# Rows of x turned by a diagonal of their norms inside the projections, and half of the output weight split before attention

## What is computed

```python
hn   = rms_norm(x, attn_norm_gain)          # x * rsqrt(mean(x*x)) * gain, per token
proj = hn @ w_in                            # 1024 x 3072: q, k, v (4 heads) and c, u, b of the conv
q, k = partial_rotary(rms_norm(q)), partial_rotary(rms_norm(k))
attn = diff_attention(q, k, v)              # two softmax maps per head, p0 - lam * p1, then norm
conv = rms_norm(b * causal_conv3(c * u), conv_out_gain)
x    = x + concat(attn, conv) @ w_out       # 1024 x 1024
x    = x + hier_moe(rms_norm(x, ffn_norm_gain))   # 32 experts, two per token
```

## Time and profile before

| | us |
|---|---|
| median of 3 runs | 1182.52 (1179.73 to 1183.26) |
| profiled execution, its own time | 1183.22 |
| profiled execution, span of the core | 1181.4 |
| PE busy | 1106.2 (94% of the span) |
| DVE busy | 841.2 (71%) |
| ACT busy | 657.1 (56%) |
| POOL busy | 354.9 (30%) |
| TensorE clock granted, mean of the span | 0.978 of full |

### The profile page before, as it was taken

The page is one execution under the profiler, slowest core; times in us unless marked ns, Lnnn a source line. Parts: engine busy times, 40 slices in busy tenths (PEclk is TensorE's granted clock), DMA queues, the critical chain, the costliest instruction groups (busy, mean ns, idle before and its releaser), DMA issues.

```text
span 1181.4 us, 15242 instructions
## 1 busy us (share of the span) xinstructions
PE 1106.2 (94%) x5629; PEld 867.1 (73%) x5629; DVE 841.2 (71%) x1110; ACT 657.1 (56%) x901; POOL 354.9 (30%) x431
## 2 busy tenths in 40 slices
PE   4999999999879999989789999999999999999995
PEld 3998989889658877767657777777777777766663
DVE  6644354343587776766669899889889889888894
ACT  5412121111366555443348778778877877777773
POOL 2432333233311111112104433344344344222220
PEclk9999999999899999999789999999999999999998
DMA  8012030300510222322789999999999999999972
GB/s 243 17 47 61 19 90 1 89 19 18 195 6 19 89 90 90 126 90 98 268 302 355 380 369 373 380 373 366 382 375 369 377 354 356 372 365 360 368 309 44
DMA packets 76506, 254.16 MB, mean 215 GB/s; under 512 B 17808, under 2 KB 42384, under 8 KB 51856
## 3 DMA queue, kind: packets, MB, share of 16 engines
q1 hardware_dynamic: 69264, 236.37, 54.0%
q0 software_dynamic: 7168, 16.79, 6.0%
HBM read 240.55 MB, written 20.97 MB: 221 GB/s over the span
## 4 chain that ended last, share of the span: by engine, by line
PE 43%; DMA 7%; DVE 3%; ACT 1%; issue 1%; POOL 0%; POOLq 0%; SPq 0%; ACTq 0%; DVEq 0%
PE banks L2070 9%; PE banks L2072 9%; PE banks L2071 9%; PE banks L2089 4%; PE banks L2091 4%; PE banks L2087 4%; DMA raw<-in_w_up 3%; DMA raw<-in_w_gate 3%; PE banks L2046 2%; DVE wlo L1991 1%; PE banks L2055 1%; DMA rows<-xn_rows,table_i 1%; ACT whi L1940 1%; DMA xn_rows<-hn 0%; PE banks L1611 0%
## 5 line engine op out<-in xcount | busy, mean ns | idle before, releaser
L1991 DVE TENSOR_TENSOR wlo<-raw,whi 128x2048 fp32r<-128x2048 f32 x190 | 428.0, 2287 | 52.2 <-ACT whi L1940 52.0
L1940 ACT CAST whi<-raw 128x2048 fp32r<-128x2048 f32 x188 | 354.0, 1910 | 39.0 <-DMA raw<-in_w_gate 23.5
L2070 PE MATMUL banks<-whi,rT_hi 128*96 128x512 f32 x512 | 206.9, 404 | 7.1 <-DVE wlo L1991 6.1
L1922 POOL DMA_INDIRECT out<-y_sb,table_i x32 | 150.5, 4702 | 198.1 <-ACT y_sb L1958 192.9
L2072 PE MATMUL banks<-whi,rT_lo 128*96 128x512 f32 x512 | 203.0, 396 | 0.0
L2071 PE MATMUL banks<-wlo,rT_hi 128*96 128x512 f32 x512 | 201.8, 394 | 0.0
L2070 PEld LDWEIGHTS banks<-whi,rT_hi 128*96 128x96 f32 x512 | 83.1, 162 | 43.2 <-DVE wlo L1991 7.2
L2072 PEld LDWEIGHTS banks<-whi,rT_lo 128*96 128x96 f32 x512 | 82.9, 162 | 36.4
L1913 POOL DMA_INDIRECT rows<-xn_rows,table_i x30 | 52.4, 1745 | 188.7 <-PE banks L2046 181.1
L2071 PEld LDWEIGHTS banks<-wlo,rT_hi 128*96 128x96 f32 x512 | 83.4, 163 | 31.4
L847 ACT ACTIVATE qk_sq<-banks 128x256 f32<-128x256 f32 x32 | 12.3, 385 | 150.0 <-PE banks L1469 150.0
(11 more groups left out here) (248 smaller groups left out, 2051.1 us busy)
## 6 DMA issues: line engine op xcount, KB each, us to landing
raw<-in_w_gate SPq DMA_DIRECT2D x64, 1024.0 KB, 22.1
raw<-in_w_up SPq DMA_DIRECT2D x64, 1024.0 KB, 22.4
raw<-in_w_down SPq DMA_DIRECT2D x64, 1024.0 KB, 23.6
c_raw<-in_w_in SPq DMA_DIRECT2D x12, 512.0 KB, 3.8
q_raw<-in_w_in SPq DMA_DIRECT2D x12, 512.0 KB, 6.0
x_stage<-in_x SPq DMA_DIRECT2D x8, 512.0 KB, 7.7
wo_raw<-in_w_out SPq DMA_DIRECT2D x2, 2048.0 KB, 10.4
h_sb<-in_x SPq DMA_DIRECT2D x8, 512.0 KB, 4.6
```

The lines of the kernel that those rows point to most:

```text
L1922: pool.indirect_dma_start(out=s.out_rows, out_offset=bass.IndirectOffsetOnAxis(ap=s.table_i[:, e:e + 1], axis=0), in_=s.y_sb[e % 2][:], in ...
L1940: act.copy(s.w_hi[i % HI][:], s.raw[i % RING][:]).then_inc(s.hi_ready, 1)
L1991: dve.tensor_tensor(s.w_lo[i % RING][:], s.raw[i % RING][:], s.w_hi[i % HI][:].bitcast(F32), ALU.subtract).then_inc(s.lo_ready, 1)
L2070: pe.matmul(o, s.rT_hi[e % 2][:, c, :], hi[:, c4, :], start=(c == 0), stop=False)
```

## The change

It does five things.

- The tile of x is turned as it is: `turn_x` multiplies the raw tile, as weights, with a diagonal matrix of 1/rms (`diag_x`, made by POOL from the identity), eight plain float32 matmuls in place of eight transposes. DVE's `normalise` is gone. The gain moves into the weights: ACT rounds `gain * w` and DVE subtracts, one instruction for each of the eight row chunks (`gain1_c[:, c]` is a scale per partition), so `round_q` and `low_q` have eight pieces of 384 columns in place of four of 768, and `round_c` and `low_c` eight of 128 in place of one of 1024.
- Only tile 0 is turned ahead of the products. Projection 0 comes first, and the PE waits for its weights chunk by chunk. Tiles 1, 2, 3, 4 and 6 are turned within projections 0 to 4, tiles 5 and 7 within units 0 and 1. One pair of PSUM banks (4 and 5) serves all turns.
- `UNIT_AFTER`: units 0 and 1 stand after projections 3 and 4, units 18 to 22 after 24 to 28; only unit 23 is left behind projection 31, split around `turn_q(0)`.
- The conv half of `w_out` is loaded after unit 22 and its four chunks are split at projections 30 and 31 and just behind; `multiply_out(0, 0)` and `(0, 1)` move from slots 4 and 5 to slots 0 and 1. The attention half is split in slots 2 to 5, one chunk in a slot.
- POOL makes the first four `q_dup` ahead of the last square; `sum_conv` writes bank 1.

```diff
-UNIT_AFTER = (-1, 2, 5, 6, 7, 7, 9, 11, 13, 14, 15, 15, 17, 19, 21, 22, 23, 23, 25, 26, 28, 29, 31, 31)
+UNIT_AFTER = (3, 4, 5, 6, 7, 7, 9, 11, 13, 14, 15, 15, 17, 19, 21, 22, 23, 23, 24, 25, 26, 27, 28, 31)
+    def turned_in(p):
+        return {0: 1, 1: 2, 2: 3, 3: 4, 4: 6}.get(p)
+    def turned_in_unit(n):
+        return {0: 5, 1: 7}.get(n)
     def fill_at(g):
+        if g < 2:
+            return 0, g
         i, q = g // HEADS - 1, g % HEADS
-        return (i, q) if 0 <= i < NT else (None, None)
+        return (i, q) if 0 <= i < NT and (i > 0 or q >= 2) else (None, None)
     def chunks_at(g):
-        return [(4, 5), (6, 7), (0, 1), (2, 3)][g - 2] if 2 <= g < 6 else ()
+        return (g - 2,) if 2 <= g < 6 else ()
...
             def rstd_x(t):
...
-                pool.tensor_tensor(s.rstd_x[:, t:t + 1], s.ss_x[:, t:t + 1], s.neg_half[:, t:t + 1], ALU.pow).then_inc(x_rstd_ready, 1)
+                own.then(pool.tensor_tensor(s.rstd_x[:, t:t + 1], s.ss_x[:, t:t + 1], s.neg_half[:, t:t + 1], ALU.pow))
+                if t >= 2:
+                    pool.wait_ge(x_turned, t - 1)
+                pool.tensor_scalar(s.diag_x[t % 2][:], ident[:], s.rstd_x[:, t:t + 1], None, ALU.mult).then_inc(diag_ready, 1)
...
             def round_c(j):
...
-                act.copy(s.c_hi[j % 2][:], s.c_raw[j % 2][:]).then_inc(c_hi_ready, 1)
+                for c in range(KC):
+                    act.activation(s.c_hi[j % 2][:, c, :], s.c_raw[j % 2][:, c, :], ACT.Identity,
+                                   scale=s.gain1_c[:, c:c + 1]).then_inc(c_hi_ready, 1)
...
             def low_c(j):
-                dve.wait_ge(c_hi_ready, j + 1)
-                dve.tensor_tensor(s.c_lo[j % 2][:], s.c_raw[j % 2][:], s.c_hi[j % 2][:].bitcast(F32),
-                                  ALU.subtract).then_inc(c_lo_ready, 1)
+                dve.wait_ge(c_hi_ready, KC * (j + 1))
+                for c in range(KC):
+                    dve.scalar_tensor_tensor(s.c_lo[j % 2][:, c, :], s.c_raw[j % 2][:, c, :], s.gain1_c[:, c:c + 1],
+                                             s.c_hi[j % 2][:, c, :].bitcast(F32), ALU.mult, ALU.subtract).then_inc(c_lo_ready, 1)
...
             def turn_x(t):
                 a, _ = x_banks(t)
-                pe.wait_ge(xn_ready, t + 1)
-                if t >= 2:
-                    pe.wait_ge(xlo_ready, t - 1 if t < 5 else t)
+                pe.wait_ge(diag_ready, t + 1)
+                if t >= 1:
+                    pe.wait_ge(xlo_ready, t)
                 for c in range(KC):
-                    ins = pe.transpose(ps[:, a + c // 4, (c % 4) * P:(c % 4 + 1) * P], s.xn[t % 2][:, c * P:(c + 1) * P], ident[:])
+                    ins = pe.matmul(ps[:, a + c // 4, (c % 4) * P:(c % 4 + 1) * P], s.x_stage[t][:, c * P:(c + 1) * P], s.diag_x[t % 2][:],
+                                    start=True, stop=True)
...
             def project(p):
...
-                pe.wait_ge(q_lo_ready, PIECES * (h + 1))
                 for c in range(KC):
+                    if t == 0:
+                        pe.wait_ge(q_lo_ready, KC * h + c + 1)
+                    if c == (4 if p == 0 else 2) and turned_in(p) is not None:
+                        turn_x(turned_in(p))
...
             pe.wait_ge(consts, 3)
-            for t in range(4):
-                turn_x(t)
-            multiply_unit(0)
+            turn_x(0)
             for p in range(PROJ):
                 project(p)
-                if p < 4:
-                    turn_x(4 + p)
...
-            multiply_unit(UNITS - 2)
             turn_k(PROJ - 2)
+            multiply_unit(UNITS - 1, (0,))
             turn_q(0)
-            multiply_unit(UNITS - 1, (0,))
+            multiply_unit(UNITS - 1, (1,))
             turn_k(PROJ - 1)
+            turn_q(1)
             for g in range(SLOTS_2):
...
-                if g == 0:
-                    turn_q(1)
-                    multiply_unit(UNITS - 1, (1,))
```

More of the change, by code:

```diff
@@ L179, in layer_kernel @@
         x_stage = [at(f"x_stage{t}", 76 + 8 * (NT - 1 - t), [P, D]) for t in range(NT)]
-        xn = [at(f"xn{b}", 72 + 8 * b, [P, D]) for b in range(2)]
-        gain1 = at("gain1", 88, [P, D])
+        diag_x = [at(f"diag_x{b}", 72 + 8 * b, [P, P]) for b in range(2)]
+        gain1_c = at("gain1_c", 3.8125, [P, KC])
         squares = at("squares", 96, [P, D])
@@ L211, in layer_kernel @@
         ma_hi = [at(f"ma_hi{b}", 172 + 2 * b, [P, HEADS, P], F32R) for b in range(2)]
[L212 to L214 removed]
+        ma_lo = [at(f"ma_lo{b}", 180 + 2 * b, [P, HEADS, P], F32R) for b in range(2)]
+        mc_hi = at("mc_hi", 176, [P, CT, P], F32R)
+        mc_lo = at("mc_lo", 178, [P, CT, P], F32R)
         h_sb = [at(f"h_sb{b}", 184 + 4 * b, [P, D]) for b in range(2)]
@@ L362, in front @@
     taps_in = sem("taps_in")
-    x_in = [sem(f"x_in{n}") for n in range(5)]
+    x_in = [sem(f"x_in{n}") for n in range(NT)]
     qw_in = sem("qw_in")
@@ L467, in units_after @@
     def units_after(p):
-        return [n for n in range(1, UNITS) if UNIT_AFTER[n] == p]
+        return [n for n in range(UNITS) if UNIT_AFTER[n] == p]
     def split_after(n):
@@ L608, in _ @@
                 sp.dma_start(s.sub_gain[:], s.subln_gain.rearrange("a p -> p a")).then_inc(small_in, 16)
-                for t in range(4, NT):
+                load_x(2)
+                load_x(3)
+                load_c(0)
+                load_x(4)
+                load_c(1)
+                for t in range(5, NT):
                     load_x(t)
-                load_c(1)
                 for m in range(CT):
@@ L790, in _ @@
                     rstd_o(g - 2)
[L791 removed]
+                if 2 <= g and g + 2 < SLOTS_2:
                     double_q(g + 2)
@@ L832, in round_q @@
                     act.wait_ge(projected, NT * h)
-                for n in range(PIECES):
-                    act.copy(piece(s.q_hi, n), piece(s.q_raw, n).rearrange("p c j n -> p c (j n)")).then_inc(q_hi_ready, 1)
+                if h == 0:
+                    act.wait_ge(gain1_in, 16)
+                for c in range(KC):
+                    act.activation(s.q_hi[:, c, :], s.q_raw[:, c, :, :].rearrange("p j n -> p (j n)"), ACT.Identity,
+                                   scale=s.gain1_c[:, c:c + 1]).then_inc(q_hi_ready, 1)
             def round_c(j):
```

223 lines of the change are left out of this document (109 added, 114 removed).

## The result

The changed kernel takes **1190.74 us** (median of 5 runs, 1188.48 to 1192.74), the kernel before 1182.38 beside it on the same chip. The ratio is 1.0072, 95% interval 1.0049 to 1.0095: slower by 0.7%, 8.4 us between the medians. A second measurement of the same kernel gave 1.0070 (1.0045 to 1.0096). The profiled execution took 1190.74 with a span of 1189.0, that is 7.6 over the profiled span of before (1181.4).

The account below looks back on a forecast made before the run. The PE was taken to bound the projections, with room for gain in the head and at the start of attention. Terms summed to +2.5 on 1183.22: 1185.7 profiled, 1185.0 median, own range 1180 to 1189, wide range 1176 to 1192.

Parts of the forecast that it names:

- Start of the products: Head: the first product starts at 14.75 instead of 24.07 us, -9.3.
- Turns: Among the products: seven turns of sixteen records each instead of four turns of 0.79, +9.3.
- First projections: Projections 0 to 3: PE waits for diagonals and low parts behind ACT's pieces, +2.6 (bounds 1 and 5).
- Tile 7: Unit 1, behind projection 4: PE waits 3.5 for the diagonal, plus 1.2 for half a chance of slow clock, +4.7.
- Conv blocks: Five units wait for low parts of conv blocks made in eight pieces, +5.1 (bounds 0 and 8).
- The rival that they do not bite: The five conv waits and tile 7's are covered, so 9.8 goes: 1175.2; chance 0.22.
- Head weights: Heads 1 to 3: by chunks, the PE no longer waits for the last piece of low weights, -3.6.
- Start of attention: From projection 31's end to slot 6's turn: 50.8 without the moved unit becomes 43.5, less give-backs, -6.3 (bounds 2 and 11).
- they only shift: Experts from 600 us on: untouched by the change, their loads start where attention ends, so they only move in time.
- The rival of the clock: PE runs at 1.2 GHz behind waits in projections 0 to 3, tile 7, slots 1 to 5: +6, 1191; chance 0.20.

Follow-up runs that it names:

- silu_first: Changed kernel with the last expert's activation on ACT and product on DVE put ahead of the split of its fifth weight tile; 1188.06 us, ratio 1.0036.
- conv_chunks: Changed kernel with conv blocks handed over by chunk, a unit waiting for each chunk's low part instead of all eight; 1187.05 us, ratio 1.0033.
- tile7_early: Changed kernel with tile 7's square right behind tile 6's on ACT, its norm and diagonal ahead of projection 4's rotation on POOL; 1187.01 us, ratio 1.0036.
- fixed: Changed kernel, diagonal kept, with tile 7's square and norm early, conv blocks by chunk, output-weight low parts later, tile 1's square earlier; 1178.35 us, ratio 0.9966.

## Why the prediction was right or wrong

The median fell in the range and on the side with the largest chance, but the predicted 1185.0 itself was 5.7 too low, and its own range ended at 1189. That the wide range held is owed to the values of the rivals that it took in.

- **Start of the products:** -9.07 for -9.3. The diagonal took 0.62 instead of 0.4, sixteen cold records to the rounding 3.5 instead of 3.6.
- **Turns:** +9.3 was right by the records (1.70 to 1.81 from start to next start for six of the seven), and with transposes the PE was busy 7.8 less on its turns. They ate the earlier start, as said.
- **First projections:** 2.0 in waits (1.31, 0.26, 0.47) for 2.6. ACT's eight pieces of 384 columns took 4.16 together, 0.52 each, and eight of 128 in a conv block 2.45, 0.31 each. The rule of the Trainium skill that the prediction weighed (ScalarE: Activation LUTs, Rules for kernel authors) gives 0.62 and 0.41. The trace agrees for how long one lasts (0.605 and 0.398 on the mean), but in a row each starts before the last one has ended, so the 0.5 of the prediction was right and the extra waits did not come.
- **Tile 7:** wait 3.59 for 3.5. The clock fell, in both profiles: 1.7, where half a chance of it was priced at 1.2. Term 5.3 for 4.7.
- **Conv blocks:** five waits at the five places, 0.90, 0.90, 0.90, 0.84, 0.90 instead of 1.15 and 1.0: 4.4 for 5.6 before the 0.5 was taken off. The rival that they do not bite falls by its own test.
- **Head weights:** -3.6, all three waits gone.
- **Left over:** the terms so far sum to +8.4 as measured, and projection 31 ends 9.5 later (310.07 against 295.12, less 5.47 for the moved unit). The 1.1 between is taken up at the end of this document.
- **Start of attention:** mis-sized. Slot 6's turn comes 46.3 behind projection 31, the working had 43.5. The waits of slots 1 to 5 were right (1.1, 1.75, 2.3, 2.0 and 2.6 for 1.1, 1.8, 2.7, 1.8 and 2.5). But the first quarter ended at +13.1 instead of +11.4: 1.0 of it is the keys of projection 30, where the prediction priced DVE's queue (0.35) and left out that POOL stands still beside those low parts; 0.7 is left over, on the PE. The other 1.1 built up in the slots, and I cannot place it. The 0.7 for the clock did not come, it was 1.00 from 310 to 360 us.
- **The step that failed** is the first paragraph's "they only shift" on the experts. They end on a chain in which ACT's fixed order puts the last activation behind a tile's landing, and this cost 1.8 for the wait and 2.5 for the clock; the experts' stretch grew by 3.5 to 3.8. That is the larger part of the 5.7. That the order decides is shown by silu_first; why the tile landed later is not, only that it does so in every kernel with the diagonal. A look at the last 30 us of the trace of before would have shown a wait of 1.78 for `hid` behind a landing, a place where a small change of times can cost.

The rival of the clock named 1191 and the number came, but not by its mechanism: it wanted slow stretches behind waits in projections 0 to 3 and slots 1 to 5, and from 310 to 360 us the clock was full. Where it was right is tile 7, tile 1's turn in projection 0 in the second profile (3.4 for 1.8) and, unnamed, the last expert.

## What to carry to other kernels

Price a step that is moved onto the bounding engine by its records there, not by what it frees elsewhere: a diagonal that saves DVE a product of 0.74 us costs the PE twice the records of a transpose. Put the work that a turn waits for (here one square on ACT) ahead in its queue wherever its data has long landed; a single square in the wrong place cost 4 to 5 us. And look at the last expert or tile of a pipeline that runs at its loads' pace: here an operation that stood in order behind a late landing decided 4 us of the end, and moved with an edit 1100 us earlier.

## What was not expected of the hardware

- POOL's add on four columns took 1.19 instead of 0.20, and its power 1.93 instead of 1.02, beside DVE's products of two inputs in SBUF.
- Stops cost a little more than their wait: the five waits sum to 4.4, but without them the first output turn of conv_chunks is 5.6 earlier. The first two products behind a stop start 0.34 apart instead of 0.23 (95.87 and 96.21), which makes 0.1 a stop; the rest I cannot place.
- Some falls of the clock stay with a kernel, others don't. In slots 1 to 2 both profiles of the changed kernel show 6.0 between output turns, while tile7_early, whose difference lies at 60 us, shows 7.2; yet fixed, which has that edit too, shows 6.0. Tile 1's turn took 1.8 in one execution of the changed kernel and 3.4 in the other.
- The end of the experts depends on how x was turned 1100 us earlier: see the last wait in the table.
